# Two decoder stacks, three attentions: exponentials scaled before they are turned, outputs produced already turned

## The reference

```python
s = jnp.where(k_pos[None, :] <= q_pos[:, None], s, -jnp.inf)   # s = q.k * scale (+ gates)
w = jax.nn.softmax(s, axis=-1).astype(v.dtype)
o = jnp.einsum('bhqk,bkhd->bqhd', w, v)
return o.reshape(B, S, D_MODEL) @ w_o
```

## Time and profile before

| | |
|---|---|
| Median of 3 runs | 1513.63 us |
| Profiled execution, first to last instruction (span) | 1511.2 us |
| Median of the runs less that span | 2.4 us |
| TensorE busy | 1493.9 us, 99% |
| VectorE busy | 920.0 us, 61% |
| ScalarE busy | 792.0 us, 52% |
| GpSimd busy | 189.9 us, 13% |
| Granted TensorE clock, mean | 0.998 |

### The profile page before, as it was taken

The page is one execution under the profiler, slowest core; times in us unless marked ns, Lnnn a source line. Parts: engine busy times, 40 slices in busy tenths (PEclk is TensorE's granted clock), DMA queues, the critical chain, the costliest instruction groups (busy, mean ns, idle before and its releaser), DMA issues.

```text
span 1511.2 us, 21617 instructions
## 1 busy us (share of the span) xinstructions
PE 1493.9 (99%) x8200; PEld 1293.6 (86%) x8200; DVE 920.0 (61%) x1192; ACT 792.0 (52%) x956; POOL 189.9 (13%) x56
## 2 busy tenths in 40 slices
PE   8999999999999999999999999999999999999997
PEld 6888888888888888898888888888888998888886
DVE  7475465666666566523776668766666455756667
ACT  5446545444444444666554456654446654544456
POOL 0014211000040000362100001000005441100010
PEclk9999999999999999999999999999999999999999
DMA  8545446655546555551565556565555434655562
GB/s 313 182 140 177 160 156 196 212 191 194 193 160 203 194 186 177 174 186 65 187 206 187 194 195 226 175 218 185 185 191 162 123 121 162 205 199 184 187 211 81
DMA packets 187258, 273.71 MB, mean 181 GB/s; under 512 B 10144, under 2 KB 137280, under 8 KB 187200
## 3 DMA queue, kind: packets, MB, share of 16 engines
q1 hardware_dynamic: 183136, 261.72, 51.6%
q10 hardware_dynamic: 4064, 11.18, 2.4%
HBM read 271.78 MB, written 1.05 MB: 181 GB/s over the span
## 4 chain that ended last, share of the span: by engine, by line
PE 94%; DVE 3%; ACT 2%; DMA 1%; issue 0%; SPq 0%; ACTq 0%; DVEq 0%
PE bank L694 23%; PE bank L696 12%; PE bank L551 8%; PE bank L553 7%; PE bank L552 7%; PE acc L551 7%; PE acc L552 7%; PE acc L553 7%; PE bank L726 3%; PE acc L853 2%; PE acc L547 2%; PE bank L608 2%; PE bank L601 2%; PE bank L616 2%; DVE tanh L1869 1%; DVE x L1890 1%
## 5 line engine op out<-in xcount | busy, mean ns | idle before, releaser
L1785 DVE TENSOR_TENSOR w_lo<-w_raw,w_hi 128x2048 fp32r<-128x2048 f32 (+2 forms) x209 | 475.2, 2278 | 163.1 <-ACT w_hi L1344 121.4
L694 PE MATMUL bank<-xT,w_hi 128*128 128x512 f32 x1520 | 380.0, 392 | 0.2 <-DVE w_lo L1785 0.2
L499 POOL TENSOR_TENSOR w_lo<-w_raw,w_hi 128x2048 fp32r<-128x2048 f32 (+1 forms) x41 | 176.7, 4316 | 1278.6 <-ACT w_hi L1262 1278.6
L694 PEld LDWEIGHTS bank<-xT,w_hi 128*128 128x128 f32 x1520 | 276.3, 189 | 52.4 <-DVE w_lo L1785 0.9
L1344 ACT ACTIVATE w_hi<-w_raw 128x2048 fp32r<-128x2048 f32 x145 | 276.4, 1907 | 0.0
L696 PEld LDWEIGHTS bank<-xT,w_lo 128*128 128x128 f32 x1520 | 207.4, 190 | 14.8
L696 PE MATMUL bank<-xT,w_lo 128*128 128x256 f32 x1520 | 211.9, 282 | 0.0
L1262 ACT ACTIVATE w_hi<-w_raw 128x2048 fp32r<-128x2048 f32 (+3 forms) x106 | 190.9, 1817 | 21.2 <-DMA w_raw<-in_w_in 11.4
L551 PE MATMUL acc<-w_hi,hTh 128*128 128x512 f32 x400 | 156.2, 391 | 0.0
L552 PE MATMUL acc<-w_lo,hTh 128*128 128x512 f32 x400 | 156.2, 391 | 0.0
L553 PE MATMUL acc<-w_hi,hTl 128*128 128x512 f32 x400 | 155.6, 389 | 0.0
(11 more groups left out here) (220 smaller groups left out, 2092.9 us busy)
## 6 DMA issues: line engine op xcount, KB each, us to landing
w_raw<-in_ffn_w_in SPq DMA_DIRECT2D x176, 512.0 KB, 4.4
w_raw<-in_ffn_w_out SPq DMA_DIRECT2D x88, 512.0 KB, 4.1
w_raw<-in_w_in SPq DMA_DIRECT2D x52, 512.0 KB, 4.6
w_raw<-in_fox_w_in SPq DMA_DIRECT2D x24, 512.0 KB, 4.5
w_raw<-in_w_ffn_gate SPq DMA_DIRECT2D x22, 512.0 KB, 4.4
w_raw<-in_w_ffn_up SPq DMA_DIRECT2D x22, 512.0 KB, 4.2
w_raw<-in_w_ffn_down SPq DMA_DIRECT2D x22, 512.0 KB, 4.1
w_raw<-in_ple_w_gate SPq DMA_DIRECT2D x16, 512.0 KB, 4.5
```

The costliest lines, as they stand in the source:

```text
L499: pool.tensor_tensor(w_lo[s][:, 0:cols], w_raw[u % RING][:, 0:cols], w_hi[s][:, 0:cols].bitcast(F32), ALU.subtract).then_inc(w_lo_done[u % ...
L694: pe.matmul(out, wh[:, k, m], both, start=k == 0, stop=False)
L1785: nc.vector.tensor_tensor(w_lo[s][:, 0:cols], w_raw[u % RING][:, 0:cols], w_hi[s][:, 0:cols].bitcast(F32), ALU.subtract).then_inc(w_lo_don ...
```

## The change

The exponentials are written to the bank of the scores instead of back to `pr`. VectorE, right after `soft(s)`, waits for them, takes the reciprocals and writes the scaled weights to `pr` (`weights`); these are what TensorE turns. `weigh` has the values of 128 columns (two neighbouring heads of width 64, or one of 128) stationary and the turned weights moving, 256 and 128 columns wide, so the output comes turned, 256 positions wide; a head of width 64 uses its 64 rows of it. Outputs go to bank 7 and, for odd heads of the second and third attention, bank 3. ScalarE's `keep_o(s-2)` writes the high part from there, VectorE's `rest_o(s-2)` the low part, which stands behind `weights(s)` and ahead of the step's filling. All transposes of outputs, their copies, and the buffers `mo`, `fo`, `mlo` are gone; the first attention's output gets its place in sTh/sTl. Some banks change: fox_k2 and fox_k3 use bank 2, fox_o1 banks 2 and 5, mla_oa0 and mla_oa1 banks 1 and 2, one transpose after the second attention bank 0. The lines that only remove old calls on ScalarE, the renamed buffers, and arguments that follow from it are left out here.

```diff
@@ -505,11 +500,22 @@
-            return {"ret": ("gated", q, t), "moba": ("o", "moba", MOBA_H - 1), "mix": ("ev", f"moba_out{q}", t),
-                    "fox": ("o", "fox", 8 * q + 7), "raw": ("ffn_out", 0, t)}.get(site, ("norm", site, t, q))
-
-
-        TURN_BANK = {4: (4, 5, 6, 7), 8: (4, 5, 6, 7), 5: (6, 7, 0, 1)}
+            return {"ret": ("gated", q, t), "mix": ("ev", f"moba_out{q}", t),
+                    "raw": ("ffn_out", 0, t)}.get(site, ("norm", site, t, q))
+
+        def head_place(name, h):
+
+            if name == "mla":
+                return slice(0, P), h
+            return slice(64 * (h % 2), 64 * (h % 2) + 64), h // 2 + (8 if name == "fox" else 0)
+
+        def out_bank(name, h):
+
+            return 7 if name == "moba" or h % 2 == 0 else 3
+
+
+
+        TURN_BANK = {3: (4, 0, 6, 7), 4: (4, 5, 6, 7), 8: (4, 5, 6, 7), 5: (6, 7, 0, 1)}
...
@@ -518,15 +524,14 @@
-        O_BANK = [2, 3, 2, 3, 2, 1, 0, 1]
-
...
-        FOX_FILL = {0: [("fox_q2", 2, 1)], 1: [("fox_k2", 3, 0)], 2: [("fox_k2", 3, 1)], 7: [("fox_q3", 2, 0)],
-                    8: [("fox_q3", 2, 1)], 9: [("fox_k3", 3, 0)], 10: [("fox_k3", 3, 1)]}
+        FOX_FILL = {0: [("fox_q2", 2, 1)], 1: [("fox_k2", 2, 0)], 2: [("fox_k2", 2, 1)], 7: [("fox_q3", 2, 0)],
+                    8: [("fox_q3", 2, 1)], 9: [("fox_k3", 2, 0)], 10: [("fox_k3", 2, 1)]}
+        FOX_BANK = (2, 5)
...
@@ -841,9 +846,9 @@
-            def attention(name, heads, qk, v, dv, fill):
+            def attention(name, heads, qk, v, fill):
...
-                    take(4 + h % 2, ("soft", name, h))
+                    take(4 + h % 2, ("weights", name, h))
...
@@ -854,17 +859,16 @@
-                    need("pe", "exp", name, h)
+                    need("pe", "weights", name, h)
...
-                    take(7, ("o", name, h))
+                    take(out_bank(name, h), ("o", name, h))
...
-                    b, p = bank[7], pT[:, h % 2]
-                    pe.matmul(b[:, 0:dv], p[:, 0:P], v(h, 0), start=True, stop=True)
-                    pe.matmul(b[:, dv:2 * dv], p[:, P:2 * P], v(h, 0), start=True, stop=False)
-                    pe.matmul(b[:, dv:2 * dv], p[:, 2 * P:3 * P], v(h, 1), start=False, stop=True)\
+                    out, p = bank[out_bank(name, h)][:, 0:S], pT[:, h % 2]
+                    pe.matmul(out, v(h, 0), p[:, 0:S], start=True, stop=False)
+                    pe.matmul(out[:, P:S], v(h, 1), p[:, S:S + P], start=False, stop=True)\
...
@@ -939,18 +943,17 @@
-                      lambda h, t: mv[:, t, h * MOBA_DH:(h + 1) * MOBA_DH], MOBA_DH,
+                      lambda h, t: mv[:, t, h // 2 * P:(h // 2 + 1) * P],
...
-            to_xT("moba", mo, (0,), b0=4)
...
-            need_xT("moba", (0,))
-            chunk("moba_out0", (0, 1))
-            moba_out1 = Chunk("moba_out1", (2, 3))
+            need("pe", "o", "moba", MOBA_H - 1)
+            chunk("moba_out0", (0, 1), src=(sTh, sTl))
+            moba_out1 = Chunk("moba_out1", (2, 3), src=(sTh, sTl))
...
@@ -1097,22 +1100,18 @@
-                        return fv[:, t, h * FOX_DH:(h + 1) * FOX_DH]
+                        return fv[:, t, h // 2 * P:(h // 2 + 1) * P]
...
-                    o0, o1 = (Chunk(f"fox_o{c}", b, ready="fox") for c, b in ((0, (0, 1)), (1, (2, 3))))
+                    o0, o1 = (Chunk(f"fox_o{c}", b, slot0=8, ready="fox") for c, b in ((0, (0, 1)), (1, FOX_BANK)))
...
-                    fill |= {11: [lambda: to_xT("fox", fo, (0,), tiles=(0,))], 12: [lambda: o0.run(0, tiles=(0,), part=0)],
-                             13: [lambda: to_xT("fox", fo, (0,), tiles=(1,)), lambda: o0.run(0, tiles=(0,), part=1)], 14: [lambda: o0.run(0, tiles=(1,))],
+                    fill |= {12: [lambda: o0.run(0, tiles=(0,), part=0)],
+                             13: [lambda: o0.run(0, tiles=(0,), part=1)], 14: [lambda: o0.run(0, tiles=(1,))],
...
-                    attention("fox", FOX_H, fox_qk, fox_v, FOX_DH, fill)
-                    for t in range(T):
-                        need("pe", *site_ready("fox", t, 1))
-                        transposes(4 + t, ("xT", "fox", t, 1), ("T", "fox", t, 1),
-                                   [(j * P, fo[:, t, (4 + j) * P:(5 + j) * P]) for j in range(4)])
+                    attention("fox", FOX_H, fox_qk, fox_v, fill)
...
@@ -1156,12 +1155,6 @@
-                    def turn_o(g):
-                        need("pe", "o", "mla", 2 * g + 1)
-                        transposes(O_BANK[g], ("oT", g), ("oTf", g),
-                                   [(j * S + t * P, mlo[:, g % 2, t, j * VD:(j + 1) * VD])
-                                    for t in range(T) for j in range(2)])
-
...
@@ -1176,27 +1169,22 @@
-                    for g in range(7):
-                        fill[2 * g + 4].append(lambda g=g: turn_o(g))
...
-                    oa = [unit_steps(f"mla_oa{c}", (3, 2)) for c in range(2)]
-                    fill[13] += [lambda: [need("pe", "oT", g) for g in range(4)], oa[0][0]]
+                    oa = [unit_steps(f"mla_oa{c}", (1, 2)) for c in range(2)]
+                    fill[13] += [lambda: need("pe", "o", "mla", 7), oa[0][0]]
...
-                    attention("mla", MLA_H, mla_qk, lambda h, t: vv[:, t, h * VD:(h + 1) * VD], VD, fill)
+                    attention("mla", MLA_H, mla_qk, lambda h, t: vv[:, t, h * VD:(h + 1) * VD], fill)
...
-                    turn_o(7)
-                    need("pe", "oT", 4)
-                    need("pe", "oT", 5)
+                    need("pe", "o", "mla", 11)
...
-                    need("pe", "oT", 6)
-                    need("pe", "oT", 7)
+                    need("pe", "o", "mla", 15)
...
@@ -1402,12 +1390,21 @@
-                        go(("exp", name, h) if t else (), pr[:, h % 2, c], pr[:, h % 2, c], ACT.Exp,
+                        go(("exp", name, h) if t else (), bank[4 + h % 2][:, c], pr[:, h % 2, c], ACT.Exp,
...
+
+                def keep_o(h):
+                    need("act", "PV", name, h)
+                    rows, k = head_place(name, h)
+                    dst = (sTh if name == "moba" else xTh)[rows, k, :]
+                    go(("oh", name, h), dst, bank[out_bank(name, h)][rows, 0:S])
+                    if name == "fox" and h % 8 == 7:
+                        for t in range(T):
+                            note(("xTh", "fox", t, h // 8), "act_done", counts["act_done"])
...
@@ -1416,6 +1413,8 @@
+                    if 2 <= s < heads + 2:
+                        keep_o(s - 2)
...
@@ -1995,7 +1984,7 @@
-            def attention(name, heads, out, dv, fill):
+            def attention(name, heads, fill):
...
@@ -2012,23 +2001,34 @@
-                def gather(h):
-                    need("dve", "PV", name, h)
+                def weights(h):
+                    need("dve", "exp", name, h)
...
-                        did(nc.vector.tensor_scalar(out(h, t), bank[7][:, t * dv:(t + 1) * dv],
-                                                    rsum[:, r + t:r + t + 1], None, ALU.mult),
-                            *(("o", name, h) if t else ()))
+                        c = slice(0, P) if t == 0 else slice(P, 3 * P)
+                        did(nc.vector.tensor_scalar(pr[:, h % 2, c], bank[4 + h % 2][:, c], rsum[:, r + t:r + t + 1], None,
+                                                    ALU.mult),
+                            *(("weights", name, h) if t else ()))
+
+                def rest_o(h):
+                    need("dve", "oh", name, h)
+                    rows, k = head_place(name, h)
+                    hi, lo = (m[rows, k, :] for m in ((sTh, sTl) if name == "moba" else (xTh, xTl)))
+                    did(nc.vector.tensor_tensor(lo, bank[out_bank(name, h)][rows, 0:S], hi.bitcast(F32), ALU.subtract), "o", name, h)
+                    if name == "fox" and h % 8 == 7:
+                        for t in range(T):
+                            note(("xT", "fox", t, h // 8), "dve_done", counts["dve_done"])
...
+                        weights(s)
+                    if 2 <= s < heads + 2:
+                        rest_o(s - 2)
...
-                    if 2 <= s < heads + 2:
-                        gather(s - 2)
...
@@ -2184,10 +2184,8 @@
-            attention("moba", MOBA_H, lambda h, t: mo[:, t, h * MOBA_DH:(h + 1) * MOBA_DH], MOBA_DH,
-                      fill)
+            attention("moba", MOBA_H, fill)
...
-            xT_evac("moba", (0,), b0=4)
...
@@ -2216,13 +2214,13 @@
-            def by_tile(stage, alpha, banks=(0, 1)):
+            def by_tile(stage, alpha, banks=(0, 1), others=(2, 3)):
...
-                    add_chunk(stage, 1, t, (2, 3), alpha)
+                    add_chunk(stage, 1, t, others, alpha)
...
@@ -2300,15 +2298,11 @@
-                    attention("fox", FOX_H, lambda h, t: fo[:, t, h * FOX_DH:(h + 1) * FOX_DH], FOX_DH,
-                              {8: [lambda: split_to(uo + 1)], 10: [lambda: split_to(uo + 2)],
-                               11: [lambda: xT_evac("fox", (0,), tiles=(0,))],
```

(30 more changed lines are left out.)

16 lines of the change are left out of this document (3 added, 13 removed).

## The result

| | before | after |
|---|---|---|
| median of 8 runs each | 1513.58 us | 1517.78 us |
| lowest to highest | 1513.44 to 1514.14 | 1517.49 to 1519.05 |
| span of the profiled execution | 1511.2 us | 1516.1 us |

The ratio is 1.0029, with a 95% interval of 1.0020 to 1.0038: the change makes the kernel 4.2 us slower, where the prediction said 1.5. A second set of runs gave 1517.33 us, ratio 1.0027 (1.0016 to 1.0038).

What follows compares the result with a forecast made beforehand. The prediction took TensorE's instruction stream to be the time. Third attention +2.8, second -0.9, first 0 and weighing -0.4 gave +1.5 us, 1515.1 us, with a range of 1510.5 to 1519.5.

Steps and rivals of the forecast that it cites:

- weighing, all heads: TensorE's products with the probabilities, in their new form: -0.4 us, between nothing and 0.8 gained over 40 heads.
- first attention: Removed transposes -0.9, step 6's transposes waiting +0.4, late low half of ret_out0's weights +0.45: sum 0.
- second attention: fox_k2's new bank +0.5, step 11 to step 13 -0.3, transposes removed after it -1.1: sum -0.9 us.
- third attention: Removed transposes -3.5, step 0 +0.5, step 14 +0.6, turn_rope waits +3.5, mla_oa1 +1.7: sum +2.8 us.
- Rival 2: Scores to weights takes longer than 4.20 us by d: 1517.3 us at d = 0.2, 1520.6 at 0.5; chance 0.22.
- What leaves TensorE: Output transposes go in all three attentions: 14 fours at 0.44 us each, 6.2 us.
- The multiplications: VectorE's scaling of the weights: 480 ns taken for 256 columns, 347 for 128; transposes can start 4.20 us after scores.
- waits for turn_rope: Third attention: TensorE waits 0.58 us for VectorE's turn_rope in steps 3, 5, 7, 9, 11 and 13, 3.5 us.
- late low half: End of the first attention: VectorE's low halves of ret_out0 stand behind rest_o(6) and rest_o(7), +0.45 us.
- Rival 1: The new waits don't arise: 1506.1 us, or 1510.6 with half of them left; chance 0.12.
- Rival 3: VectorE's weight splitting falls behind after the first and second attention, three-buffer ring starves once: 1518 us; chance 0.08.
- Rival 4: Scaling finishes while transposes wait anyway for ScalarE's copy, so four places cost nothing: 1513.2 us; chance 0.08.

Runs made afterwards that it cites:

- c: The changed kernel with turn_rope of groups 2 to 7 one step earlier on VectorE, nothing else: 1513.46 us, ratio 1.0000.
- g: The changed kernel with turn_rope one step earlier, weighing ahead of transposes, fox_k2 in bank 1, and the third attention's filling ahead of rest_o: 1510.40 us, ratio 0.9978.
- j: As g, but with the weighing put back behind the transposes in all three attentions: 1510.89 us, ratio 0.9984.
- d: The changed kernel without the multiplications, exponentials into SBUF as before, outputs left unnormalised: 1513.65 us, ratio 1.0001.
- h2: The kernel before with exponentials to PSUM, multiplications ahead of the transposes, and gather between soft and weights on VectorE: 1524.14 us, ratio 1.0068.
- e: The changed kernel with the weighing ahead of the transposes on TensorE in all three attentions: 1517.51 us, ratio 1.0027.
- i2: The kernel before with turn_rope alone one step earlier on VectorE: 1515.00 us, ratio 1.0008.

## Why the prediction was right or wrong

Offsets below are the ends of matched TensorE records after, less before, in the profiled executions; each stage is its own difference.

| stage | predicted | measured |
|---|---|---|
| weighing, all heads | -0.4 | in the stages (about 0.02 a head in the first two, none seen in the third) |
| first attention | 0 | +1.2 |
| before the first feed-forward | 0 | +1.1 (+0.1 in the repeat) |
| second attention | -0.9 | -1.1 |
| third attention | +2.8 | +3.6 |
| sum | +1.5 | +4.8 (+3.7 without the chance term) |

The measured 1517.78 us lie within the stated range, 1510.5 to 1519.5, and the kernel is slower, as forecast. They lie outside the forecast's own 1513 to 1517, and the loss is 4.2 us where 1.5 was said: nearly three times. Rival 2 names 1517.3 us, closer than the forecast, by a mechanism that the trace doesn't have. The kinds of wait were foreseen; what was off are sizes in the first and third attention, and one term of the first that was put at nothing.

**What leaves TensorE: right.** No transposes of outputs are left (L547 before, L552 now); the 14 fours are gone.

**The multiplications: right.** 475 ns for 256 columns against 480 taken on the slope, and 351 for 128. They end 4.15 us after the scores of the step shown above, against 4.16 (groups of VectorE: count | busy, mean ns | idle before):

```profile
L2011 DVE TENSOR_SCALAR arena<-acc,exp_rsum 128x256 f32<-128x256 f32 x40 | 19.0, 475 | 0.0
...
L2011 DVE TENSOR_SCALAR arena<-acc,exp_rsum 128x128 f32<-128x128 f32 x40 | 14.0, 351 | 1.4
```

The row decided rightly against the Trainium skill (VectorE: DVE Perf Modes, The TRN2 errata), by whose formula 256 columns take an estimated 0.39 us. What the Trainium skill (ScalarE: Activation LUTs, Step-by-step: what each stage is for) says of the PSUM side agrees in sign: the exponentials of 256 columns take 460 ns into PSUM against 494 before.

```profile
L1258 ACT ACTIVATE acc<-arena,negmax 128x256 f32<-128x256 f32 x40 | 18.4, 460 | 0.0
```

**The third attention: right in every mechanism, short in one size.** Step 0 costs 0.6 (predicted 0.5), step 14 0.66 (0.6), mla_oa1 1.8 (1.7), and the removal of each turn_o brings 0.44 to 0.49. The waits for turn_rope are the term that was sized too small: five cost 0.72 us each and the last, of mla_oa0, 0.65, where 0.58 stood in the sum: 0.8 us in all. In the steps shown it is 6.32 us from scores to uq (1199.79 to 1206.11); without turn_o it was 5.59. I had the end of turn_rope at 6.21 after the scores (measured 6.17), but 0.04 us from there to TensorE's record, where it is 0.15 (1205.96 to 1206.11), and I had allowed uq's first record a start 0.08 later, which it doesn't have. Two allowances of a tenth of a microsecond, taken six times. Why this handover takes 0.15, where the one at 1249.97 below takes 0.05, stays open. c confirms the size: without the six waits its third attention is 4.3 us shorter in the trace, against the 4.2 above, and the kernel 3.9 us faster. The other waits, of steps 0 and 14 and of mla_oa1:

```profile
1188.72 0.55 PE L552 MATMUL acc<-ident,arena 128*128 128x128 f32 x3 [0.36 <-DVE arena L2011]
...
1249.97 0.55 PE L552 MATMUL acc<-ident,arena 128*128 128x128 f32 x3 [0.44 <-DVE arena L2011]
...
1259.18 0.50 PE L556 MATMUL bank<-w_hi,xT 128*128 128x512 f32 x1 [1.53 <-DVE x L1824]
```

**The second attention: right**, +0.58 for fox_k2 (predicted 0.5) and -1.1 in all. In step 11, with its filling gone, the transposes stand 1.19 us:

```profile
704.11 0.55 PE L552 MATMUL acc<-ident,arena 128*128 128x128 f32 x3 [1.19 <-DVE arena L2011]
```

**The first attention: this step failed.** It said "Filled with 6 us steps except step 6" and priced only that step and the late low half, so that with the removal of 0.9 the stage came to 0; it costs 1.2. Three things were missed or too small. Step 0:

```profile
126.99 4.45 DVE L2180 SCALAR_TENSOR_TENSOR arena<-squares,neg_mean,arena 128x512 f32<-128x512 f32 x2
131.35 0.28 DVE L2000 CUSTOM_DVE_ANT_0 arena<-acc,mask 128x128 f32<-128x128 f32 x1
...
133.24 0.74 DVE L2011 TENSOR_SCALAR arena<-acc,exp_rsum 128x128 f32<-128x128 f32 x2
```

Rows of the same times stand in the trace before: VectorE comes to the first `soft` only at 131.35, behind the gated product (L2180) of the retention branch, so step 0 has its slack spent already: +0.53, a term that the sum put at nothing. The steps after it give 0.14 back by the shorter weighing. Step 6 cost 0.95 where 0.41 stood. The exponentials of head 6 start at 165.79 where they started at 164.91 before, 0.5 later than the offset there accounts for: ScalarE has keep_o, 0.38 us at 162.29, in front of its split of weights and of the filling, where nothing stood before. The late low half cost 0.76 where 0.45 was priced:

```profile
184.93 0.50 PE L556 MATMUL bank<-w_hi,xT 128*128 128x512 f32 x1 [0.57 <-DVE w_lo L1774]
```

What makes the last 0.3 us of it wasn't isolated by a run.

**The rivals.** Rival 1 (waits don't arise) is refuted by the list of waits. Rival 2's mechanism, weights late by d, isn't there: the multiplications end where priced. Rival 3 (the ring starves) didn't show: behind the attentions the low half is late once, by 0.6 us. The prediction's sign for it, TensorE short of w_lo for more than a microsecond, did appear: 1.25 us before 252.89. But this wait follows a DMA's issue, and is 0.3 in the repeat (last section). Rival 4 (the way isn't longer) falls with the waits at 1188.72 and 1249.97 in the two places named for it. The chance of slower by over 0.2% was 0.26, and slower by 0.28% is what came. The prediction remarked that with the two additions ahead of rest_o the 1.7 us would be 0; in g and j that wait is gone. What it didn't ask is whether turn_rope itself could move, the largest term.

## What to carry to other kernels

Work taken off the engine that sets the time is gained only as far as nothing else was due at the end of it: here turn_o's transposes were also cover for VectorE's turn_rope. In d, where they are gone and the multiplications too, the 6 us that this frees are spent in waits behind rest_o and for banks. When a change puts a wait in the middle of an in-order queue, list what is queued behind it and move the item with a deadline in front of the wait; one such line was worth 3.9 us, all that was lost. Look first at which bank the moved item then delays: the same line costs the kernel with one bank for the outputs 1.4 us.

## What the runs showed of the hardware

**A wait can cost twice.** In h2 TensorE idles 1.98 us before 706.00:

```profile
706.00 1.22 PE L601 MATMUL bank<-w_hi,xT 128*128 128x512 f32 x2 [1.98 <-DVE xT L1825]
```

From near the end of this wait on it is granted half clock. Windows of h2 (the window, its length, busy time of PE, PEld, DVE, ACT and POOL with the number of instructions, then the granted clock as a share of full, share of the DMA engines, GB/s):

```profile
705.00:706.00 1.00, 0.00 (x0) 0.00 (x1) 0.94 (x2) 1.00 (x1) 0.00 (x0) 0.85 0.00 0
706.00:707.00 1.00, 1.00 (x2) 0.83 (x3) 0.00 (x0) 0.55 (x1) 0.00 (x0) 0.50 0.00 0
...
708.00:709.00 1.00, 1.00 (x5) 0.82 (x4) 0.00 (x0) 0.00 (x0) 0.00 (x0) 0.50 0.00 0
709.00:710.00 1.00, 1.00 (x9) 0.90 (x8) 0.23 (x3) 0.00 (x0) 0.00 (x0) 0.94 0.00 0
```

0.50 is the lower level, 1.2 of 2.4 GHz, for about 3.1 us of work, so that some 1.6 us are lost beside the 2.0 of the wait. The same follows the wait of 2.39 us in h2, and in e the one of 1.92 us for add_chunk (windows of e):

```profile
1259.00:1260.00 1.00, 1.00 (x3) 0.80 (x4) 0.49 (x2) 0.62 (x1) 0.00 (x0) 0.59 0.06 20
1260.00:1261.00 1.00, 1.00 (x3) 0.76 (x3) 0.00 (x0) 0.00 (x0) 0.00 (x0) 0.50 0.55 154
```

Of e's 11 executions four have a mean granted clock of 0.997 and take 1519.10 to 1519.45 us; the other seven have 0.998 or 0.999 and take 1516.90 to 1517.64, some 2 us less. By these clocks the same program meets the fall in some executions and not in others. The kernel after, whose wait in that place is 1.53 us, keeps full clock there, and so does the kernel before after its wait of 4.96 us at the very start. What decides it was not measured.

**The issue of one DMA on ScalarE's queue** took 1.53 us in the profiled execution of the kernel after, and 0.46 in its repeat and in the kernel before; ScalarE's split of the next weights starts that much later, and TensorE waits 1.3 us instead of 0.3. Nothing of the change touches it. Over all 14 profiled executions it took 0.46 us in eleven, 0.57 in i2, 1.16 in g, whose trace has a wait of 1.2 us behind it, and 1.53 here. What lengthens it stays open.

```profile
246.96 1.53 ACTq L1323 DMA_DIRECT2D rope_ret<-in_p  x1
```
